# MoBA key and query heads turned inside the third projection chunk, keys normed doubled, one projection group behind each attention step

## The reference

```python
h = rms_norm(x, norm1_g[l])
proj = h @ w_in[l]                       # 1024 x 2560
r_q, r_k, r_v, r_g, m_q, m_k, m_v, c_q = jnp.split(proj, SPLIT_POINTS, axis=-1)
ro = retention(rotary(r_q), rotary(r_k) * 64 ** -0.5, r_v)     # 4 heads
y_ret = silu(r_g) * rms_norm(ro, ret_norm_g[l])
mq = rms_norm(split_heads(m_q, 4), moba_qn_g[l])               # heads of 64
mk = rms_norm(split_heads(m_k, 4), moba_kn_g[l])
y_moba = moba_attention(mq, mk, m_v)
mem_kv = rms_norm(mem, mem_norm_g[l]) @ w_mem_kv[l]
ck = rms_norm(mem_kv[..., :256], mem_kn_g[l])                  # per head
cq = rms_norm(split_heads(c_q, 4), mem_qn_g[l])
y_mem = memory_attention(cq, ck, mem_kv[..., 256:])
x = x + concat(y_ret, y_moba, y_mem) @ w_out[l]
x = x + hier_moe(rms_norm(x, norm2_g[l]), ...)                 # 16 experts, top 2 in the top group
```

## Time and profile before

| | |
|---|---|
| time, median of 3 runs | 1203.28 us (1201.59 to 1205.28) |
| the profiled execution's own time | 1203.65 us |
| its span | 1201.9 us |
| PE busy | 1103.8 us, 92% |
| DVE busy | 903.4 us, 75% |
| ACT busy | 723.1 us, 60% |
| POOL busy | 162.8 us, 14% |
| mean granted TensorE clock | 0.96 |

### The profile page before, as it was taken

One profiled execution on the slowest core, in us unless ns is written; L12 is line 12 of the kernel. 1 busy time (PEld: TensorE's weight loads), 2 busy tenths in 40 slices (PEclk: granted clock), 3 DMA queues, 4 the chain that ended last, 5 costly groups with the idle time before them and its releaser, 6 DMA issues.

```text
span 1201.9 us, 18008 instructions
## 1 busy us (share of the span) xinstructions
PE 1103.8 (92%) x5538; PEld 920.7 (77%) x5538; DVE 903.4 (75%) x1314; ACT 723.1 (60%) x1011; POOL 162.8 (14%) x238
## 2 busy tenths in 40 slices
PE   4999799999999999999489988989999999999990
PEld 3887698788788888888368868878788888888870
DVE  5458766738999999998484586764579999999973
ACT  6325433424888888888442263333368898888860
POOL 2000222001010110120400005010011111111011
PEclk9999889999999999999789998999999999999995
DMA  9522201217999979998953202112199997999965
GB/s 345 174 89 70 70 25 56 88 53 260 373 382 377 366 262 385 377 383 323 330 184 88 88 35 71 45 53 103 66 338 379 373 375 272 355 379 387 383 245 220
DMA packets 121872, 277.26 MB, mean 231 GB/s; under 512 B 13265, under 2 KB 13473, under 8 KB 121680
## 3 DMA queue, kind: packets, MB, share of 16 engines
q1 hardware_dynamic: 106912, 240.30, 55.1%
q0 software_dynamic: 14896, 36.19, 8.2%
HBM read 269.56 MB, written 23.07 MB: 243 GB/s over the span
## 4 chain that ended last, share of the span: by engine, by line
PE 75%; DVE 12%; DMA 6%; issue 3%; ACT 2%; POOL 0%; POOLq 0%; DVEq 0%; SPq 0%; ACTq 0%
PE bank L1428 21%; PE bank L1430 20%; PE bank L1429 20%; PE bank L1460 2%; DMA stage<-in_w_exp_up 2%; PE bank L1764 2%; DVE w_lo L403 1%; PE bank L1557 1%; PE bank L1563 1%; DVE w_lo L407 1%; PE bank L1783 1%; DMA hd<-pair_rows 1%; PE bank L1621 1%; PE bank L1667 1%; DVE x L954 1%
## 5 line engine op out<-in xcount | busy, mean ns | idle before, releaser
L403 DVE TENSOR_TENSOR w_lo<-stage,w_hi 128x1024 fp32r<-128x1024 f32 x244 | 293.6, 1220 | 11.9 <-ACT w_hi L398 4.0
L398 ACT ACTIVATE w_hi<-stage 128x1024 fp32r<-128x1024 f32 x236 | 246.4, 1059 | 44.1 <-PE bank L1430 37.6
L1428 PE MATMUL bank<-w_hi,hT_hi 128*128 128x512 f32 x384 | 158.1, 412 | 4.0 <-DVE hT_lo L968 4.0
L1430 PE MATMUL bank<-w_hi,hT_lo 128*128 128x512 f32 x384 | 152.3, 397 | 0.0
L1429 PE MATMUL bank<-w_lo,hT_hi 128*128 128x512 f32 x384 | 152.3, 397 | 0.0
L403 DVE TENSOR_TENSOR more_lo<-stage,more_hi 128x1024 fp32r<-128x1024 f32 x124 | 146.3, 1217 | 4.1 <-ACT more_hi L398 3.1
L398 ACT ACTIVATE more_hi<-stage 128x1024 fp32r<-128x1024 f32 x124 | 128.0, 1062 | 17.2 <-PE bank L1430 12.6
L366 ACT ACTIVATE w_hi<-stage 128x1024 fp32r<-128x1024 f32 x56 | 58.8, 1058 | 100.3 <-PE bank L1430 100.3
L407 DVE TENSOR_TENSOR w_lo<-stage,w_hi 128x1024 fp32r<-128x1024 f32 x56 | 69.4, 1248 | 64.4 <-ACT w_hi L366 62.9
L1428 PE MATMUL bank<-w_hi,xgT_hi 128*128 128x512 f32 x264 | 104.0, 394 | 1.1 <-DVE xgT_lo L1328 1.1
L1430 PE MATMUL bank<-w_hi,xgT_lo 128*128 128x512 f32 x264 | 103.7, 393 | 0.0
(11 more groups left out here) (266 smaller groups left out, 2051.8 us busy)
## 6 DMA issues: line engine op xcount, KB each, us to landing
stage<-in_w_exp_up SPq DMA_DIRECT2D x124, 512.0 KB, 7.1
stage<-in_w_exp_gate SPq DMA_DIRECT2D x122, 512.0 KB, 7.1
stage<-in_w_exp_down SPq DMA_DIRECT2D x122, 512.0 KB, 7.0
stage<-in_w_in SPq DMA_DIRECT2D x40, 512.0 KB, 4.1
stage<-in_w_out SPq DMA_DIRECT2D x16, 512.0 KB, 4.0
stage<-in_w_mem_kv SPq DMA_DIRECT2D x8, 512.0 KB, 9.9
h_scratch<-act POOLq DMA_DIRECT2D x8, 512.0 KB, 3.0
act<-pair_rows POOLq DMA_DIRECT2D x8, 512.0 KB, 6.2
```

The source lines that it names most:

```text
L398: eng.activation(x_hi[n % NX], src, ACT.Copy).then_inc(s_hi, 1)
L403: eng.tensor_tensor(x_lo[n % NX], src, x_hi[n % NX].bitcast(f32), ALU.subtract).then_inc(s_lo, 1)
L1428: pe.matmul(dst, l_hi, r_hi, start=start, stop=False)
L1430: return pe.matmul(dst, l_lo, r_hi, start=False, stop=stop)
```

## The change

- Keys are normed one tile of 256 columns at a time for queries (in place) and for keys, whose gain multiplication writes each head twice side by side (`twice`, into the free half of `act`, for the memory keys into `probs`). A transposed 128-column block of keys then holds one head in both halves of the partitions.
- Four key turns, one per head, stand in the third projection chunk, behind its tenth group (units 12 and 13 and two tiles of unit 14), into banks 4 to 7; the two MoBA query turns stand behind unit 14, into banks 4 and 5. The memory keys and queries are turned after unit 16, into banks 0 to 3. A key bank is copied and subtracted in one operation of 128x512 each; queries stay in halves of 64 partitions.
- On ACT and DVE the conversions of units 16 to 19 stand between these pieces. `TURN_BANK` names the banks.
- Three groups ahead of the loop instead of six, one behind each of steps 0 to 24, none behind step 25. Chunk 1 is evacuated one tile at a time behind jobs 6 to 9. Units 22 and 23 are converted behind jobs 5 and 10 instead of 2 and 5.

```diff
-FILL_FIRST = 6
-AFTER_STEP = [1] * 6 + [0] * 4 + [1] * 16
-FREED_AT = {0: 0, 1: 1, 2: 2, 5: 3, 13: 4, 17: 5, 21: 6, 23: 7}
+FILL_FIRST = 3
+AFTER_STEP = [1] * 25 + [0]
+FREED_AT = {0: 0, 1: 1, 5: 2, 10: 3, 13: 4, 17: 5, 21: 6, 23: 7}
+        TURN_BANK = (4, 5, 6, 7, 4, 5, 0, 1, 2, 3)
...
@@ ACT
-                for n in range(3):
+                def heads_hi(j, dst):
+                    sc.wait_ge(s_tq, j + 1)
+                    sc.activation(dst, bank[TURN_BANK[j]][:, :], ACT.Copy).then_inc(s_tqh, 1)
...
+                make_hi(sc, base, 16)
+                make_hi(sc, base, 17)
+                for h in range(H):
+                    heads_hi(h, mk_hi[:, h, :])
+                sc.wait_ge(s_tq, 6)
+                for g in range(2):
+                    queries_hi(4 + g, mq_pair(g))
+                head_roots(2)
+                make_hi(sc, base, 18)
+                make_hi(sc, base, 19)
+                evacuate(2)
+                for g in range(2):
+                    heads_hi(6 + g, ck_hi[:, 2 * g:2 * g + 2, :].rearrange("p i c -> p (i c)"))
+                sc.wait_ge(s_tq, 10)
+                for g in range(2):
+                    queries_hi(8 + g, cq_both[2 * g:2 * g + 2])
...
-                    if j == 5:
-                        evacuate(3)
+                    if 6 <= j < 6 + NT:
+                        evacuate(3, [j - 6])
...
@@ DVE
+                        chain(dv.tensor_tensor(twice.rearrange("p (h d c) -> p h d c", h=H, d=2),
+                                               bc(v3.unsqueeze(2), [128, H, 2, DH]),
+                                               bc(g_head[:, gain, :].unsqueeze(1).unsqueeze(1), [128, H, 2, DH]),
+                                               ALU.mult))
...
+                for k in range(4):
+                    make_lo(dv, base, 12 + k)
+                dv.wait_ge(s_stdq, 1)
+                chain(dv.reciprocal(rstdq[:, 0:32], rstdq[:, 0:32]))
+                for t in range(NT):
+                    head_norm(pq[3][:, t, 0:256], 8 * t, 0)
+                    head_norm(pq[3][:, t, 256:512], 8 * t + 4, 1, twice=act[:, t, 512:1024])
+                dv.sem_inc(s_qn, 1)
+                dv.wait_ge(s_mkve, 2)
+                for t in range(2):
+                    head_squares(ck[:, t, 0:256], 4, ssq[:, 48 + 4 * t:52 + 4 * t])
+                for t in range(NT):
+                    dv.wait_ge(s_pev, 4 + t + 1)
+                    head_squares(pq[4][:, t, 256:512], 4, ssq[:, 32 + 4 * t:36 + 4 * t])
+                dv.sem_inc(s_ssq, 1)
+                for h in range(H):
+                    heads_lo(h, mk_lo[h], mk_hi[:, h, :])
+                make_lo(dv, base, 16)
+                make_lo(dv, base, 17)
+                for g in range(2):
+                    queries_lo(4 + g, mq_pair(g))
+                dv.wait_ge(s_stdq, 2)
+                chain(dv.reciprocal(rstdq[:, 32:56], rstdq[:, 32:56]))
+                for t in range(2):
+                    head_norm(ck[:, t, 0:256], 48 + 4 * t, 3, twice=probs[:, t, :])
+                for t in range(NT):
+                    head_norm(pq[4][:, t, 256:512], 32 + 4 * t, 2)
+                dv.sem_inc(s_qn, 1)
+                make_lo(dv, base, 18)
+                make_lo(dv, base, 19)
+                for g in range(2):
+                    heads_lo(6 + g, ck_lo[g], ck_hi[:, 2 * g:2 * g + 2, :].rearrange("p i c -> p (i c)"))
 +                for g in range(2):
+                    queries_lo(8 + g, cq_both[2 * g:2 * g + 2])
...
@@ PE
-                for n in range(3):
-                    project(n)
+                project(0)
+                project(1)
...
+                pe.wait_ge(s_pev, 4)
+                third(0)
+                third(1)
+                third(2, 0)
+                third(2, 1)
+                pe.wait_ge(s_pev, 8)
+                pe.wait_ge(s_qn, 1)
+                for h in range(H):
+                    turn_key(h)
+                for t in range(2, NT):
+                    third(2, t)
+                for g in range(2):
+                    pe.wait_ge(s_tqe, g + 1)
+                    turn(lambda q: pq[3][:, q, 128 * g:128 * g + 128], TURN_BANK[4 + g], s_tq)
+                third(3)
+                pe.wait_ge(s_tqe, 6)
                 rows(hT_hi, hT_lo, base, 16, 0, (4, 5, 6, 7))
...
                 pe.wait_ge(s_pev, 12)
-                pe.wait_ge(s_qn, 1)
-                for j in range(4):
-                    turn(lambda q: pq[3][:, q, 128 * j:128 * j + 128], j, s_tq)
-                for g in (4, 5):
+                pe.wait_ge(s_qn, 2)
+                for g in range(2):
+                    for i in range(2):
+                        for t in range(2):
+                            col, h = 256 * i + 128 * t, 2 * g + i
+                            ins = pe.transpose(bank[TURN_BANK[6 + g]][:, col:col + 128],
+                                               probs[:, t, 128 * h:128 * h + 128], ident)
+                    ins.then_inc(s_tq, 1)
+                for g in range(2):
+                    turn(lambda q: pq[4][:, q, 256 + 128 * g:256 + 128 * g + 128], TURN_BANK[8 + g], s_tq)
+                for g in range(4, 4 + FILL_FIRST):
                     fill(g)
...
+                pe.wait_ge(s_tqe, 10)
```

More of the change, by code:

```diff
@@ L337, in __call__, with mq_pair @@
                 self.eng.wait_ge(self.s, self.n)
+        def mq_pair(g):
+            return [mq_both[:, 2 * g + i, :].rearrange("p (t c) -> p t c", t=NT) for i in range(2)]
         def bc(ap, shape):
@@ L732, in _, with evacuate @@
                     sc.activation(cv[:, t, :], bank[4 + t][:, 256:512], ACT.Copy).then_inc(s_mkve, 1)
-                def evacuate(n):
-                    for t in range(NT):
+                def evacuate(n, tiles=range(NT)):
+                    for t in tiles:
                         if t < NT - 1:
@@ new lines, in queries_lo @@
+                def queries_lo(j, pair):
+                    dv.wait_ge(s_tqh, j + 1)
+                    for i in range(2):
+                        ins = dv.tensor_tensor(pair[i][half[1 - i], :, :], bank[TURN_BANK[j]][half[i], :]
+                                               .rearrange("p (t c) -> p t c", t=NT),
+                                               pair[i][half[i], :, :].bitcast(f32), ALU.subtract)
+                    ins.then_inc(s_tqe, 1)
+                for k in range(4):
+                    make_lo(dv, base, 8 + k)
@@ L1081, in _ @@
                 for g in range(2):
-                    heads_lo(5 + g, [(cq_both[2 * g + i][half[1 - i], :, :],
-                                      bank[1 + g][half[i], :].rearrange("p (t c) -> p t c", t=NT),
-                                      cq_both[2 * g + i][half[i], :, :]) for i in range(2)])
+                    queries_lo(8 + g, cq_both[2 * g:2 * g + 2])
                 def probs_out(j):
@@ L1490, in project, with turn_key, third @@
                              done=s_proj)
-                for n in range(3):
-                    project(n)
+                project(0)
+                project(1)
+                def turn_key(h):
+                    turn(lambda q: act[:, q, 512 + 128 * h:640 + 128 * h], TURN_BANK[h], s_tq)
+                def third(j, only=None):
+                    rows(hT_hi, hT_lo, base, 12 + j, j, (0, 1, 2, 3), s_proj, only=only)
+                pe.wait_ge(s_pev, 4)
+                third(0)
+                third(1)
@@ L1591, in _ @@
                 ins.then_inc(s_r, 1)
-                pe.wait_ge(s_tqe, 11)
+                pe.wait_ge(s_tqe, 14)
                 def ret_scores(r):
```

117 lines of the change are left out of this document (33 added, 84 removed).

## The result

| | before | after |
|---|---|---|
| median (each beside the other) | 1202.68 us (1201.59 to 1205.28, 4 runs) | 1185.35 us (1183.23 to 1185.77, 4 runs) |
| ratio, 95% interval | | 0.985 (0.983 to 0.987) |
| the profiled execution | 1203.65 us | 1185.31 us |
| its span | 1201.9 us | 1183.4 us |
| mean granted TensorE clock | 0.96 | 0.97 |

The change gained 17.3 us where 21.0 were forecast; 1185.35 lies in the range, 3.1 us above the forecast of 1182.3, so just outside its narrow band of 3 us. Of the 45 executions of before in all batches one, slow, took 2816.97 us; it stands in no median here.

The account below looks back on a forecast made before the run. PE, busy 92% of the span, was taken as the bound: 17.3 us of waits plus 14.1 of lower clock, 31.4, less 10.4 of new costs, gives back 21.0, so 1182.3 us; range 1175 to 1194.

Parts of the forecast that it names:

- narrow band of 3 us: Whole execution: a measured median within 3 us of the forecast 1182.3 us, given a chance of 0.57.
- The DVE layout: Third chunk to loop: DVE's queue decides; laid out from 80.0, it has the loop start at 118.0 us in layer 0.
- The new waits: PE's new idle per layer: 2.1 us ahead of the loop, 0.6 in it, 1.2 at the first turn behind it.
- The clock's term: Ahead of and in the loop, both layers: 14.1 us lost to the lower clock, all to be given back.
- at 2.4 GHz that work takes half: PE's busy time in the four stretches at clock 0.50 would halve at full clock, giving 14.1 us.
- the filled steps: Loop steps 6 to 9, formerly without a group, become full-clock steps with one, leaving PE no idle moment.
- That half-height operations are the cost: Ahead of the loop: half-height copies and subtractions cost as much as full ones; doubling cuts them from 20 to 14 per engine.
- the six rivals: Clock falls (0.13), DVE slips (0.09), filled steps no shorter (0.05), better (0.10), doubled write slower (0.03), only the region shorter (0.03).
- rival 2: Ahead of the loop: DVE slips, doubled writes at 1.38 us add 4.1 us a layer, 1190.5 us; chance 0.09.
- rival 1: The clock still falls: ahead of the loop costs 4.1 us (1186), in the loop as well 14.1 (1196); chance 0.13.
- The split under the rotary: Step 12: unit 23's split falls under POOL's rotary, taking 1.99 us against 1.22; PE waits 0.3 us.
- What follows moves up as it is.: Behind the loop in each layer, retention, output projection and experts are released by PE's progress and move up unchanged.

Follow-up runs that it names:

- the keep-busy run: The kernel before with unread 512-column matmuls added in PE's waits ahead of the loop and of the turns of steps 7 to 10: 1200.50 us, ratio 0.998.
- the loop-alone run: The kernel before with only three groups ahead of the loop, one behind each of steps 0 to 24, tile-wise evacuation and later conversions: 1199.64 us, ratio 0.998.
- the paired keys: The changed kernel with keys not doubled, two heads to a key turn, four half-height copies and subtractions per key bank: 1199.46 us, ratio 0.996.
- the better order: The changed kernel with the splits of units 17, 18 and 19 later in DVE's queue: 1179.72 us, ratio 0.979; timed again 1180.45 us, 0.981.
- its variant: The better order with one more group moved from ahead of the loop to behind step 25 (two ahead, 26 behind steps): 1185.22 us, ratio 0.984.
- the turns alone: The changed kernel with the old distribution of groups: six ahead of the loop, six behind steps 0 to 5, whole evacuation: 1190.99 us, ratio 0.992.

## Why the prediction was right, and where it was not

**The DVE layout held.** The prediction had the key turns 12.5 us and the loop 36.9 us behind the root; they came 12.4 and 36.56 behind it. (The key turns come with PE's own work; of DVE's queue itself, the norms were to be done 10.1 and the memory norms 30.1 us behind the root, and were done at 10.0 and 29.7.) The doubled write cost what was taken. DVE's and ACT's groups of after (busy, mean ns):

```profile
L1036 DVE TENSOR_TENSOR proj<-proj,rstdq 128x256 f32<-128x256 f32 x12 | 5.1, 424 | 0.4
...
L1040 DVE TENSOR_TENSOR act<-proj,g_head 128x512 f32<-128x512 f32 x4 | 2.8, 692 | 0.1
...
L1057 DVE TENSOR_TENSOR mk_lo<-bank,mk_hi 128x512 fp32r<-128x512 f32 x3 | 1.9, 685 | 0.2 <-DVE ssq L1031 0.2
```

```profile
L751 ACT ACTIVATE mk_hi<-bank 128x512 fp32r<-128x512 f32 x4 | 2.1, 603 | 2.1 <-PE bank L1483 2.1
```

0.692 us, the price of the nearest row; a full-height subtraction took 0.685 and a copy 0.603, the half-height ones 0.687 and 0.592.

**The new waits were somewhat smaller.** Per layer, forecast and measured in layer 0: 0.2 us and none before unit 16; memory norms 1.1 and 0.72; loop start 0.8 and 0.54; first step 0.3 and 0.18; step 12 0.3 and none, but 0.21 at step 8 (137.72), which I had not seen; tail 1.2 and 1.02. Together 3.9 and 2.67. With the transposes the cost was 4.0 instead of 5.2 us a layer.

**The clock's term was too large, by about as much.** Layer 0's region went from 117.61 to 106.51 us; PE's idle time in it from 8.76 (117.61 - 108.85 busy) to 2.74 us (106.51 - 103.77 busy). The lines are the region's stretch in either kernel, before and after:

```profile
81.06:198.67 117.61, 108.85 (x592) 94.31 (x591) 83.80 (x166) 51.78 (x116) 20.93 (x23) 0.93 0.19 61
```

```profile
81.80:188.31 106.51, 103.77 (x605) 89.15 (x603) 81.09 (x164) 49.06 (x112) 21.32 (x23) 1.00 0.21 67
```

Idle fell by 6.0 us where the forecast's terms give 4.75 (8.65 in waits less 3.9). Busy time fell by 5.1 us where they give 6.4 (half of 15.36 less 1.25 for the transposes). The step that was mis-sized is "at 2.4 GHz that work takes half": a matmul of 512 columns in a group takes 0.427 us from start to start at 0.50 (before, 122.6 to 129.4) and 0.227 at 1.00 (before, 82 to 92), so not quite half (nor twice as long, as said ahead of the rows), and the 15.36 us lose 7.2, not 7.7. The other 0.8 us of the difference I can't place.

Nor does all that PE loses reach the region. The four profiles of before price the lower clock themselves: layers with 13.7 us at 0.50 in the region take 116.2 to 116.4 us, those with 17.1 take 117.5 to 118.0, those with 20.5 take 118.4 and 118.5, that is 0.32 us for each us at the lower clock. Carried down to none, on the 30.7 us of the first profile, that is as an estimate 10 us for both layers instead of 14.1, and the keep-busy run fits it (7.1 us, with up to 3.4 for its unread matmuls). That others than PE set some of those steps is likely but not shown. The errors cancel: what the clock gave less, the shorter waits and the filled steps gave more, and the regions gave 21.1 us for 21.0. That closeness is luck.

**The ingredients of the argument.** That DVE sets the loop's start: shown by the doubled write issued twice (4.3 us in, 4.4 us out) and by the loop-alone run (unchanged 43.17). That the filled steps run without waiting: shown, 32.83 of 33 us. That half-height operations are the cost: shown by the paired keys, and the effect is larger than I had it: DVE's idle time of 0.96 and 1.97 us behind four copies a bank adds to its extra operations. None of the six rivals happened (of rival 2 the path is real, the price did not occur); of rival 1, no fall came in the region in any of the seven profiles without a wait over 2.2 us there (after twice, the better order twice, its variant, the doubled write issued twice, PE kept busy).

**The split under the rotary.** I had DVE at 1.99 us a second time, at step 12. The overlap came there (that step's scores start at 148.00), but the other way round. Timeline of after:

```profile
147.47 1.22 DVE L411 TENSOR_TENSOR w_lo<-stage,w_hi 128x1024 fp32r<-128x1024 f32 x1
...
147.50 2.15 POOL L592 TENSOR_TENSOR act<-proj,con 128x512 f32<-128x512 f32 x1
```

DVE began 0.03 us sooner and took its plain 1.22; POOL's multiplication took 2.15 instead of 1.09. The Trainium skill (SBUF — State Buffer, Who interferes with whom) has such pairs exclude each other for whole instructions: these rows agree in the main, POOL losing 1.06 us while DVE had 1.19 to go, and the earlier trace rows shows the other side. PE had no wait at step 12; the 0.21 us at step 8 stand behind unit 22's split (DVE, 134.40), ahead of that job's maximum.

**"What follows moves up as it is."** This is where forecast and measurement part. The profiled executions differ by 18.3 us, 21.1 in the regions less 2.8 outside: 0.7 more ahead of the first root (81.06 and 81.80), 1.4 in the experts' stages (nearly all in layer 0, where a fall of the clock lasted 6.8 us instead of 3.4), 0.6 between them and layer 1's root, 0.1 between turns and experts. None of these comes back: the first root stands at 78.9 in the second profile of after and at 79.2 to 82.0 in three of before, the experts' stage of a layer takes 290.8 to 293.7 us whatever the kernel, and outside the regions before has 969.7 to 971.7, after and its better order 966.8 to 972.5. So that cost is not shown to be one of the change.

By medians a gap stays: 17.3, or 18.2 with all 44 executions of before (1203.5) and all eight of after (1185.35), against 21 to 22 in the regions. If the regions are taken as they were in the profiles (234.7, 212.8 and, for the better order, 210.6), the mean outside them over all executions is, as an estimate, 969.1 us in before (44), 972.6 in after (8) and 969.8 in the better order (10). So after spends some 3 us more outside, and the better order, which contains the change, does not. What moves there is in the main the clock (last section), but why it costs after more is open.

## What to carry to other kernels

Ahead of a loop that one in-order queue must prepare, lay out that queue operation by operation from a fixed event: its sum sets the start, and work shifted between the two sides of the start on another engine changes nothing but the length of its wait. An operation over half the partitions cost as much as one over all of them, and a consumer waits for the last of the pieces, so the gain of writing data doubled once lies in the wait it shortens as much as in the operations it saves. Order each queue by who is waited for first, splits of far-off weights last: that was worth a further 2 us in the regions here, for three splits moved.

## What the runs showed of the hardware

**A clock that falls with PE never idle.** From the turns behind the loop to the experts all kernels run the same code, and yet a layer takes 93.4, 95.0, 96.6 or 98.2 us for it. The second profile of after, layer 0, where it took 98.3 (PE's timeline):

```profile
239.76 0.39 PE L1451 MATMUL bank<-w_hi,hT_hi 128*128 128x512 f32 x1
239.98 0.39 PE L1452 MATMUL bank<-w_lo,hT_hi 128*128 128x512 f32 x1
...
240.44 1.86 PE L1707 MATMUL bank<-wg,hd 128*128 128x20 f32 x16
242.14 2.55 PE L1707 MATMUL bank<-wg,probsT 128*128 128x20 f32 x16
...
245.52 0.63 PE L1453 MATMUL bank<-wx_hi,hT_lo 128*128 128x512 f32 x1
245.95 0.63 PE L1451 MATMUL bank<-wx_hi,hT_hi 128*128 128x512 f32 x1
```

Ahead of the 32 router matmuls of 20 columns a 512-column matmul starts every 0.22 us, behind them every 0.43. In the first profile of after the same happens in the same place (stretches with PE busy throughout; the columns are those of the earlier trace rows):

```profile
243.40:247.50 4.10, 4.10 (x36) 3.98 (x35) 0.39 (x3) 0.00 (x0) 0.00 (x0) 1.00 0.02 6
247.50:250.90 3.40, 3.40 (x10) 2.62 (x9) 3.02 (x26) 0.00 (x0) 0.00 (x0) 0.50 0.00 0
```

In before, layer 0, the stretch of the same small matmuls (PE busy throughout as well), at full clock and with no fall behind it until 283.0:

```profile
253.70:257.20 3.50, 3.50 (x33) 3.46 (x32) 0.00 (x0) 0.00 (x0) 0.00 (x0) 1.00 0.02 5
```

There it was layer 1 that had the fall (846.24 to 849.65).

**What a fall costs.** Each layer has a second fall a little later in this part, of one length or its double (283.04 to 286.45 in before, 271.42 to 278.25 in after). The whole part, in layers 0 and 1 of before and layer 0 of the second profile of after:

```profile
198.67:292.08 93.41, 87.29 (x542) 74.75 (x541) 57.66 (x168) 31.35 (x52) 4.14 (x6) 0.98 0.28 101
786.57:883.17 96.60, 90.47 (x543) 77.52 (x541) 57.66 (x168) 31.37 (x52) 3.97 (x6) 0.95 0.29 104
```

```profile
185.31:283.56 98.25, 92.10 (x542) 78.94 (x542) 57.63 (x168) 29.80 (x50) 4.16 (x6) 0.93 0.28 100
```

In all 28 layers profiled the time follows the time at 0.50 within 0.1 us: 93.4 to 93.5 us with 3.4 us of it, 94.9 to 95.0 with 6.8, 96.5 to 96.6 with 10.2, 98.2 to 98.3 with 13.7. So each us at the lower clock costs 0.47 us here, which is what 0.227 for 0.427 us a matmul gives. Over both layers the part took 190.0 us in before and 190.1 in after, 194.9 in the second profile of after, 194.7 in the keep-busy run and 193.2 in the doubled write issued twice, and 186.8 and 187.0 with the turns alone and the paired keys, which had no fall behind the router. That is 8 us between kernels for code that none of the edits touches, and may be part of the spread of up to 9.6 us between executions of one kernel. What decides in which layer it comes, no run shows.

**Where it fell in the region, and where not.** In or behind waits of 3.2 us and more, and behind those of 2.73 and 0.59 us with bare steps around them, the clock fell in every profile; behind 1.02, 0.72 and 0.54 us in after, behind 1.4 us with two groups ahead, and behind 1.6 and 2.2 us with the doubled write issued twice, it fell in none.
